# Entry of the mixture of experts in a two-layer decoder: transposes and router moved ahead of the shared products, the ranking sent early, three weight units fetched in advance, and the second group of experts ranked

## The reference, cut to what matters

```python
x = layer_norm(DN_ALPHA * x + mix, *ln1[layer])
x = layer_norm(DN_ALPHA * x + moe(x, *moe_p[layer]), *ln2[layer])

def moe(x, router_w, router_bias, exp_w_gate, exp_w_up, exp_w_down, sh_w_gate, sh_w_up, sh_w_down):
    s = jax.nn.sigmoid((t @ router_w).astype(jnp.float32))
    ...
    def expert_step(acc, p):
        wg, wu, wd, g = p
        hid = jax.nn.silu(t @ wg) * (t @ wu)
        return acc + (hid @ wd) * g[:, None].astype(t.dtype), None
    ...
    shared = (jax.nn.silu(t @ sh_w_gate) * (t @ sh_w_up)) @ sh_w_down
```

## Time and profile before

| what | value |
|---|---|
| median of 3 runs | 1298.6 us |
| the profiled execution's own time | 1296.64 us |
| its span (first to last instruction) | 1294.9 us |
| TensorE busy | 1070.7 us (83%) |
| DVE, ACT, POOL busy | 416.4, 259.7, 80.2 us |
| DMA moved | 447.78 MB, mean 346 GB/s |
| the chain that ended last | PE 49%, DMA 42%, issue 3%, DVE 2% |
| mean granted TensorE clock | 0.936 of full |

### The profile page before, as it was taken

How to read it: one execution, slowest core, us unless ns; L and a number is a source line. 1 busy time by engine, 2 the same in 40 slices (tenths; PEclk the granted TensorE clock), 3 DMA queues, 4 the chain that set the end, 5 groups by cost and what they waited for, 6 DMA issues and landing times.

```text
span 1294.9 us, 19611 instructions
## 1 busy us (share of the span) xinstructions
PE 1070.7 (83%) x7616; PEld 650.2 (50%) x7616; DVE 416.4 (32%) x993; ACT 259.7 (20%) x619; POOL 80.2 (6%) x106
## 2 busy tenths in 40 slices
PE   7988999887978876766599999998979788767663
PEld 4764845553635434433388857455535254334331
DVE  2585632322222322111322326323222222221113
ACT  3463321111212111111023323221111121111110
POOL 1453100000000000000240000000000000000000
PEclk9989899998989898888799999999989899988887
DMA  9172499999999999999971253899999999999994
GB/s 351 61 292 98 188 369 387 397 422 420 420 422 420 420 421 421 422 422 420 360 236 66 93 233 130 352 392 395 421 420 420 421 421 421 420 422 421 423 421 171
DMA packets 78964, 447.78 MB, mean 346 GB/s; under 512 B 7579, under 2 KB 20311, under 8 KB 29734
## 3 DMA queue, kind: packets, MB, share of 16 engines
q1 hardware_dynamic: 75840, 439.25, 83.2%
q0 software_dynamic: 1904, 6.46, 1.4%
q10 hardware_dynamic: 1142, 1.01, 0.2%
HBM read 445.61 MB, written 1.05 MB: 345 GB/s over the span
## 4 chain that ended last, share of the span: by engine, by line
PE 49%; DMA 42%; issue 3%; DVE 2%; SPq 2%; ACT 1%; ACTq 0%; DVEq 0%; POOL 0%; POOLq 0%
DMA ring<-in_l_exp_w_up 33%; PE bank L1057 12%; PE bank L1183 10%; DMA ring<-in_l_exp_w_gate 7%; PE bank L905 5%; PE bank L833 4%; PE bank L970 2%; PE bank L1080 2%; PE bank L908 2%; PE bank L776 2%; SPq L612 2%; PE bank L1025 1%; DMA mixT<-in_l_conv_w 1%; PE bank L1161 1%; PE bank L1092 1%
## 5 line engine op out<-in xcount | busy, mean ns | idle before, releaser
L1183 PE MATMUL bank<-ring,big 128*32 128x256 f32 x2816 | 192.0, 435 | 97.0 <-DMA ring<-in_l_exp_w_up 64.1
L1183 PEld LDWEIGHTS bank<-ring,big 128*32 128x32 f32 x2816 | 116.3, 124 | 167.3 <-issue 127.3
L1057 PE MATMUL bank<-ring,big 128*64 128x512 f32 x640 | 151.7, 628 | 30.9 <-DMA ring<-in_l_exp_w_up 30.9
L1057 PEld LDWEIGHTS bank<-ring,big 128*64 128x64 f32 x640 | 49.4, 144 | 117.6 <-issue 115.9
L1211 PE MATMUL bank<-ring,big 128*32 128x512 f32 x704 | 86.1, 630 | 18.0 <-DMA ring<-in_l_exp_w_down 16.7
L1970 DVE TENSOR_TENSOR mixT<-mixT,bank 128x512 f32<-128x512 f32 x128 | 84.6, 684 | 29.2 <-PE bank L1161 16.9
L1949 DVE TENSOR_TENSOR big<-big,bank 128x256 f32<-128x256 f32 x22 | 9.3, 421 | 253.0 <-PE bank L1183 253.0
L1452 ACT ACTIVATE ys_high<-bank,gcol 128x512 fp32r<-128x512 f32 x84 | 57.7, 687 | 158.8 <-PE bank L1211 100.8
L1092 PE MATMUL bank<-pick,xs_high 128*128 128x128 f32 x352 | 83.4, 280 | 0.0
L2078 POOL TENSOR_TENSOR rstd<-rstd,half 128x1 f32<-128x1 f32 x10 | 13.3, 1334 | 1111.2 <-DVE rstd L1542 1111.2
L1092 PE MATMUL bank<-pick,xs_low 128*128 128x128 f32 x352 | 81.3, 275 | 0.0
(11 more groups left out here) (287 smaller groups left out, 1391.1 us busy)
## 6 DMA issues: line engine op xcount, KB each, us to landing
ring<-in_l_exp_w_gate SPq DMA_DIRECT2D x128, 1024.0 KB, 14.5
ring<-in_l_exp_w_up SPq DMA_DIRECT2D x128, 1024.0 KB, 17.6
ring<-in_l_exp_w_down SPq DMA_DIRECT2D x116, 1024.0 KB, 19.1
ring<-in_l_w_in SPq DMA_DIRECT2D x12, 1024.0 KB, 12.3
ring<-in_l_w_out SPq DMA_DIRECT2D x8, 1024.0 KB, 5.1
ring<-in_l_exp_w_down SPq DMA_DIRECT2D x16, 512.0 KB, 14.8
ring<-in_l_w_in SPq DMA_DIRECT2D x4, 1440.0 KB, 15.1
lead<-in_l_exp_w_down SPq DMA_DIRECT2D x4, 1024.0 KB, 11.2
```

The source lines that it names most:

```text
L1057: ins = mm(ps[SLOTS * q:SLOTS * q + SLOTS, :], xg[:, c, SLOTS * j:SLOTS * j + SLOTS], both[:, c], start=(c == 0), stop=(c == C - 1))
L1183: ins = mm(ps[r, 0:HID], xn[:, c, r], loop_weights(L, j, w)[:, c, :], start=(c == 0), stop=(c == C - 1))
```

## The change

It does the following, in both layers.

- **PE order.** Only two of the four shared products of block 0 stay ahead of the second transposes; the router follows at once, its second half waiting for block 1's columns; ACT and DVE copy in the order that this needs. Two shared products of block 0 and two of block 1 come behind the router, the last two of block 1 (m = 1) move behind `sort` in the middle of group 0. The eight gathers of group 0 run first and gate and up of experts 0 and 1 after them, no longer interleaved.
- **Ranking.** DVE ranks before chunk 5 is copied; PE sends `order` through PSUM after two chunks of the first gate and up (`ranked`), DVE writes it before the sorted rows, and SP reads it before the first refill.
- **Order of groups.** Group 1 is now narrow and ranked; the natural experts 4 to 7 are group 2 (wide). Wide and narrow alternate from group 0 to group 8; the numbers of groups stay 5 wide and 11 narrow.
- **Units in advance.** Gate and up of expert 3 of group 0 go to `in_big`, a place over `big` that is free after the last scores, so they are loaded before the mixer ends and not after the shared products; the two ring units beside them are loaded with group 1's weights once the shared products have read them. `LEAD` has three down units for group 2: two in `par` (loaded when the layer norm is done) and one in `xrow`.
- **Halves.** Units (0,0), (0,1), (1,0), (1,1) of group 1 are loaded in two halves of 512 KB, the first after half of the chunks (`first_half`).
- **POOL.** Three parameter broadcasts for layer 1 move from the entry of layer 0's mixture to the start of layer 1, in front of `decay_rows`; the router weights of layer 1 are loaded later, since `silS` now lies over `rw`.

The core of the diff:

```diff
+KINDS = (("first", "wide", "narrow", 1), ("back0", "narrow", "wide", 1),
+         ("turn0", "wide", "narrow", 1), ("back1", "narrow", "wide", 1),
...
-PLACE = (0, 1, 5, 2, 6, 3, 7, 4, 8, 9, 10, 11, 12, 13, 14, 15)
+PLACE = (0, 5, 1, 6, 2, 7, 3, 8, 4, 9, 10, 11, 12, 13, 14, 15)
-LEAD = [(GE - 2, 2), (GE - 1, 2)]
+IN_YS = [(GE - 1, 0), (GE - 1, 1)]
+LEAD = [(1, 2), (2, 2), (3, 2)]
+LED = BEGIN["turn0"]
...
-        lead = over("lead", "xrow", 0, [P, 2 * UNIT], F32)
+        lead_rows = over("lead_rows", "xrow", 0, [P, UNIT], F32)
+        lead_par = over("lead_par", "par", 0, [P, 2 * UNIT], F32)
+        in_big = over("in_big", "big", 2048, [P, 2 * UNIT], F32)
...
-                            mix, mix, ("ag", 3), sgu, sgu, ("ag", 3)]
-                    early = (0, 1, 8, 11, 2, 3, 4, 5, 6, 7, 9, 10)
+                            mix, mix, ("ag", 3), ("score", 0, H0 - 1), ("score", 0, H0 - 1), ("ag", 3)]
+                    early = (0, 1, 8, 11, 2, 3, 9, 10, 4, 5, 6, 7)
...
+                sp.wait_ge(S("ln_done"), 4 * L + 2)
+                for j, w in LEAD[1:]:
+                    load_lead(j, w)
                 sp.wait_ge(S("xs"), 2 * L + 2)
                 sp.wait_ge(S("acc_begun"), TB * (L + 1))
+                load_lead(*LEAD[0])
+                first, second, third = (ExpertLoop(L, kind, banks, S, bank, i=0) for kind in ALONE[:3])
                 sp.wait_ge(S("order"), L + 1)
-                experts = in_place(second.next_place())
-                refill(first, experts, LEAD)
-                refill(second, experts, in_ring)
+                experts = in_place(first.next_place())
+                sp.wait_ge(S("first_half"), L + 1)
+                for h in range(2):
+                    if h:
+                        first.read(sp, ("gu", 0))
+                    part = slice(C // 2 * h, C // 2 * h + C // 2)
+                    for j, w in IN_HALVES:
+                        sp.dma_start(loop_weights(L, j, w)[:, part, :], expert_weights(L, experts[j], w)[:, part, :])\
+                          .then_inc(S(f"unit_full{loop_unit(L, j, w)[0]}"), 16)
+                refill(first, experts, [(2, 0), (2, 1)])
+                bank_read(sp, ("sgu", L, 1))
+                for j, w in IN_YS:
...
+                refill(first, experts, IN_ORDER[2 * GE:])
+                refill(second, [GE + j for j in range(GE)], [piece for piece in BY_KIND if piece not in LEAD])
+                experts = in_place(third.next_place())
+                refill(second, experts, LEAD)
+                refill(third, experts, [piece for piece in IN_ORDER if piece not in LEAD])
...
+                def ranked(lp):
+                    pe.wait_ge(S("perm"), L + 1)
+                    ps = lp.open(pe, "ranked")
+                    mm(ps[0:1, 0:NE], expert[0:NE], perm[0:NE, 0:NE], start=True, stop=True)
...
                 for c in range(1, C, 2):
+                    if c == 5:
+                        ranks()
                     gathered(bank_read, bank_done, ("gather", L, c))
...
-            pool.wait_ge(S("ln_done"), 2)
-            for k, name in enumerate(("b_out", "ln1_g", "ln1_b")):
-                params(1, k, name)
-
-            bank_read(pool, ("router", 0))
-            pool.wait_ge(S("taken"), 1)
+            bank_moved(pool, ("sgu", 0, 1))
             router(1)
...
-            for k, name in ((3, "ln2_g"), (4, "ln2_b")):
+            for k, name in enumerate(("b_out", "ln1_g", "ln1_b", "ln2_g", "ln2_b")):
                 params(1, k, name)
```

187 lines of the change are left out of this document (106 added, 81 removed).

## The result

| what | before | after |
|---|---|---|
| median | 1297.17 us (4 runs, 1295.15 to 1299.62) | 1284.55 us (4 runs, 1283.83 to 1285.65) |
| ratio to before, 95% interval | | 0.9892 [0.9872, 0.9913] |
| the profiled execution's own time, its span | 1296.64, 1294.9 us | 1284.34, 1282.5 us |
| mean granted TensorE clock | 0.936 | 0.935 |
| the chain that ended last | PE 49%, DMA 42% | PE 53%, DMA 38% |

Faster by 12.6 us, or 14.0 by the estimate of the ratio, which is not the quotient of the two medians; 15.8 was forecast. 1284.55 lies 1.8 us over the predicted 1282.8, inside the range. It is that near only because the kernel before also came out 1.4 us lower than the 1298.6 that the forecast started from.

The account below looks back on a forecast made before the run. Bound by TensorE's products to a boundary near 237 us (886 in layer 1), then DMA transfers. -8.7 - 8.7 + 0.6 + 1.0 = -15.8 us, median 1282.8; 1275 to 1288 as a rule, range 1274 to 1293.

Parts of the forecast that it names:

- When the gathers start: Layer entries: first gathers at 156.2 us in layer 0, 5.4 us earlier; 806.0 in layer 1, about 4.3 earlier.
- Group 0: TensorE's span from first gathers on: 37.3 us before, 1.3 saved, 3.7 added for two shared products, ending at 195.9.
- Rival A: TensorE gives back half: gate and up waits for copies, group 0 4 us longer a layer; 1290.8 us, chance 0.15.
- First hole: DMA idle 11.5 us in layer 0, from 155.8 to 167.3, while SP waits for `order` before group 1's loads.
- Second hole: DMA idle 5.0 us from 197.2 us in layer 0, until group 1 has read its gates and freed a unit.
- Third hole: DMA idle 0.8 us from 254.5 us in layer 0, until group 3's last gate is read and refilled.
- Rival B: No change: idle time only moves, the third hole opens by 8 us a layer; 1298.6 us, chance 0.06.
- Fewer bytes: Expert 3's gate and up fetched before the mixer ends, 5.0 us less a layer; layer 0's three broadcasts 3.7 us less.
- (a) Halves: Group 1's 512 KB half loads at 395 GB/s against 421: cost 0.3 us a layer, at most 0.7.
- (b) `decay_rows`: Layer 1's loads behind six broadcasts, not three: cost 1.0 us, at most 9.6; by ring order 1 to 3 us late.
- The sum: Idle time and bytes spared less idle left: 8.7 us less in each layer, before costs of 0.6 and 1.0.
- Rival C: Slower: TensorE at 1.2 GHz through gathers and first gate and up in both layers; 1305.2 us, chance 0.08.

Follow-up runs that it names:

- e7: Changed kernel with the shared expert's down products and their additions before the ninth group instead of behind it: 1283.60 us, ratio 0.9902.
- e8: Changed kernel with group 3's refill loading, pair by pair, two gates then two ups instead of gate, up, gate, up: 1280.30 us, ratio 0.9880.
- e9: Changed kernel with the edits of e7 and e8 and the three moved broadcasts issued behind the `decay_rows` loads: 1276.14 us, ratio 0.9821.
- e12: e9 with TensorE's wait in front of group 2 filled by products whose result is overwritten: 1275.06 us, ratio 0.9817.
- e3: Changed kernel with expert 3's gate and up loaded behind the mixer's end again: 1286.73 us, ratio 0.9920.
- e5: Changed kernel with four units of group 1 loaded whole after the first gate and up, instead of eight halves from its middle: 1286.28 us, ratio 0.9921.
- e11: e9 with the first refill in whole units in place of 512 KB halves: 1278.03 us, ratio 0.9836.
- e10: The changed kernel itself, unaltered, timed once more on the same chip as e9: 1285.10 us, ratio 0.9901.
- e4: Changed kernel with one down unit in advance (into `xrow`) in place of three: 1289.12 us, ratio 0.9946.
- e2: Changed kernel with the router put back behind block 0's other two shared products: 1297.44 us, ratio 1.0000.

## Why the prediction was right, and where it was off

*When the gathers start.* Forecast 156.2 in layer 0 (bounds 156.1 to 157.3), measured 154.61: outside by 1.5 us. The router ran without a pause to 146.8, where 148.1 was allowed for ACT's copies, and from its end to the gathers it took 7.8 us, as in layer 1 before (8.0), not 9.2. The 9.2 us came from a stretch that was partly at the low clock. Layer 1: 797.2; the forecast 806.0 did not count the 8.3 us that all before it comes earlier. From the same starting point it is 4.8 us earlier, against 4.3.

*Group 0.* Forecast 37.3 - 1.3 + 3.7 = 39.7 us, measured 154.61 to 193.3, 38.7. Rival A (4 us more) falls.

*First hole.* Forecast 11.5 us, from 155.8 to 167.3; measured 11.3, and that they agree is luck. SP's first half went out at 163.84 (165.1 less the 1.6 us that the gathers were early makes 163.5), and bytes moved from 165.0, 1.2 us behind the issue where I had 2.2. So 9.0 us of the hole are idle DMA; the other 2.3 are the low rate of the halves, up to 174.

*Second hole.* Forecast 5.0, measured 1.7. Its start was right: the twelve units began 2.3 us early (165.0) and the halves took 2.3 us too long, which makes 197.2 again; the rate falls from 197.5 on. Its end came early: group 1's gates start at 194.44, not 196.4, SP's refill stands at 198.15, not 200.0, and bytes follow it sooner than the 2.2 us allowed.

*Third hole.* Forecast 0.8, measured 3.4 and 5.0. This is the step that failed. A hole spared earlier brings the queue sooner to its end: idle from about 253.0, not 254.5. And its refill comes later: group 2 began at 218.10, not 217.1, and took 15.65 us, not 14.2, at a clock of 0.50 for some of it; so group 3's last gate was there at 250.25, not 249.5, and the DMA at rate again near 256.4, not 255.3. 1.5 + 1.1 + 0.8 = 3.4. In layer 1 TensorE waited 4.14 us for that gate and then ran at the low clock. Rival B had the place right (the third hole opens) and the size wrong (8 us a layer; it was 2.6 and 4.2 more than forecast). The traces of e7, e8, e9 and e12 show both causes, the order of the units and the clock.

*Fewer bytes.* The 5.0 us a layer for expert 3 were booked in full. e3 puts them at 1.1 a layer, within the noise: the first hole's end does not depend on them. In my sum the term was set against a hole whose length I had computed with them, so the sum stood; as a cause it was wrong.

*A cost not seen.* The down products of the shared expert came to lie between the ninth group, now wide, and the tenth, narrow, 7.03 us of TensorE in front of the next gates. Before, the ninth was narrow as well, and the DMA ran at 419 GB/s there. Priced at nothing without a look at the order there; measured 1.7 us in layer 0 and 2.4 in layer 1 by the slices (32.1 x (1 - 390/421)), and gone in e7.

*Costs.* (a) Halves: I took 0.3 us a layer from a row at 395 GB/s, at most 0.7; they cost 2.3 us of DMA time a layer, at 312 and 324 GB/s. It did not show in the time, since they also went out 2.5 us sooner than whole units do in e5. The Trainium skill, "DMA: Bandwidth & Descriptors" (Rules for kernel authors), asks for 1 MiB or more per DMA for the full rate. Here the trace agrees: 312 GB/s in DMAs of 512 KB, 421 in DMAs of 1 MiB. (b) `decay_rows`: forecast 1.0, measured 1.49 us of wait, and 8.45 - 7.3 = 1.15 us of the lead at the start of layer 1 lost by the end of its mixer (1.0 of it is back at the transposes behind, 779.35 for 787.68). The size is near and the working wrong: I gave each broadcast 3.2 us and had six end near 671; the last of them took 13.1 us where the last of three took 9.6, and landed near 657.5, before the small loads were issued at 658.44. Those landed in 5.7 us where they took 4.0. The Trainium skill, "DMA: Bandwidth & Descriptors" (Queues, rings and completion order), has one ring worked through in order. That can't be what made the small loads late here, since the last broadcast had landed before them; that the wait came out inside my 1 to 3 us is luck.

*The sum.* Layer 0: 8.7 forecast less 0.3 for the halves, 8.45 measured. By the holes it is 17.3 + 3.7 + 5.0 - 17.0 - 1.7 = 7.3 (17.0 is all that the rate lacks from 154 to 258 us, at 352 GB/s on average; 16.4 of it lie in the three holes); 1.1 us of it I can't place. Layer 1: 8.4 less 1.0 forecast, 12.4 - 8.45 = 4.0 measured, by the holes 21.0 + 5.0 - 19.0 - 2.4 - 1.15 = 3.5, or 4.6 if the lost lead that came back is not counted. So the miss is layer 1's, 3.4 us: its third hole (4.2 more than forecast) and `shared_down` (2.4), less what the second hole spared (2.6). In layer 0 the same two came to 4.3 us, and the second hole spared 3.3. The range does not follow from its terms: their upper ends (4, 0.8, 8.6 and 2 us) add up to 15.4 us over the forecast, 1298, where it has 1288 "as a rule" and 1293.

*Rival C.* The low clock did not come where the rival put it, from 156 to 196 us (1.00 in both rows). It came behind TensorE's waits in front of groups 2 and 3, and cost 1.7 us there in layer 0. The Trainium skill, "TensorE: Matmul & The Clock Gate" (Why this matters for your kernels), warns of gaps beyond some 3 us. It agrees with the rows at 3.74, 4.14 and 5.09 us. But in layer 1 group 2 took 15.65 us behind a wait of 2.09 (e9, e11) and 15.59 behind 1.64 (e10), while in layer 0 of e3 it took 13.95 behind 2.98; so the length of the one wait does not decide it.

## What to carry to other kernels

Where a chain hands over between one engine and a DMA queue, as here, a hole closed early let the queue run ahead and opened the next one: follow the frees two groups further than the place of the change, and load a pair's units in the order in which the products read them (here both gates, then both ups). A load that already falls into a hole whose end is set by something else gains little by going out earlier still (e3); one that comes into the hole from behind it gains, and gave half of it back in the next hole (e4). Before splitting a load to start it sooner, read the rate while only the split loads are in flight, not over a stretch that mixes them with others. After any change of the order of forms, look at every unit of work that stood between two groups, here `shared_down`.

## What was not expected of the hardware

Low clock is not a matter of the kernel alone: of e9's five executions one had a mean clock of 0.935 and 1279.70 us, the others 0.940 to 0.942 and 1273.29 to 1276.34. Group 2's 64 instructions in layer 0 took 13.95 us in the traces of e3, e5, e7 and e8 and 15.65 to 16.81 in the seven others without filling, the changed kernel's two among them; a hole read from one such trace can be off by that much. The length of the wait in front does not sort them: 2.53 to 2.98 us in those four, 2.94 us in e2, which took 16.81 (what was expected of e12 had left e2 out). With the pause filled by products whose result is thrown away (2.76 us of them) the clock was at 1.00 in the one trace taken.

The halves of group 1 moved at three quarters of the rate of whole units with the DMA engines equally busy. Of the 770 packets from 164 to 174 us in the changed kernel 767 were under 8 KB, of the 335 in e5 31 were. That the size of the packets is the cause is not shown.
